# Turning the convolution's channels later: nine groups of transposes moved to the attention steps with few keys

## The reference, cut to what matters

```python
def conv_branch(u_ext, w, b, ln_g, ln_b):
    y = lax.conv_general_dilated(u_ext, w[:, None, :], ...) + b
    mu = jnp.mean(yf, axis=-1, keepdims=True)
    var = jnp.mean(jnp.square(yf - mu), axis=-1, keepdims=True)
    yn = (yf - mu) * lax.rsqrt(var + LN_EPS) * ln_g + ln_b
    return jax.nn.silu(yn)

mix = jnp.concatenate([conv_y * jax.nn.silu(gc), attn_o * jax.nn.silu(ga)], axis=-1)
out = x + mix @ w_out
```

## Time and profile before

| | |
|---|---|
| median of 3 runs | 1781.35 us |
| the profiled execution | 1779.65 us, its span 1778.0 us |
| PE busy | 1519.6 us, 85% of the span |
| DVE busy | 1042.7 us, 59% |
| ACT busy | 722.2 us, 41% |
| POOL busy | 487.1 us, 27% |
| mean granted clock of TensorE | 0.936 of full speed |
| third stage | about 957 to 1551 us of the span |

### The profile page before, as it was taken

The page is one execution under the profiler, slowest core; times in us unless marked ns, Lnnn a source line. Parts: engine busy times, 40 slices in busy tenths (PEclk is TensorE's granted clock), DMA queues, the critical chain, the costliest instruction groups (busy, mean ns, idle before and its releaser), DMA issues. The chain is left out here.

```text
span 1778.0 us, 28489 instructions
## 1 busy us (share of the span) xinstructions
PE 1519.6 (85%) x10637; PEld 1298.0 (73%) x10637; DVE 1042.7 (59%) x2135; ACT 722.2 (41%) x1302; POOL 487.1 (27%) x334
## 2 busy tenths in 40 slices
PE   5888999928979789999279999999999987549998
PEld 5786999927978669999257777776766765438886
DVE  2434999838988879898514444445544555343432
ACT  4445322224222252222124555556565654445431
POOL 2120333601434703355231011011223233141321
PEclk9999999969999899999668999999999998869999
DMA  7722442140346501232363034311121122294542
GB/s 241 223 74 48 101 120 74 47 86 30 90 136 224 162 1 49 68 103 68 113 179 85 21 90 109 70 40 33 44 67 42 53 67 66 75 228 143 167 149 98
DMA packets 183119, 172.72 MB, mean 97 GB/s; under 512 B 58974, under 2 KB 155366, under 8 KB 182462
## 3 DMA queue, kind: packets, MB, share of 16 engines
q1 hardware_dynamic: 180286, 165.14, 32.9%
q10 hardware_dynamic: 1672, 3.67, 1.3%
q0 software_dynamic: 1024, 2.10, 0.4%
HBM read 109.35 MB, written 58.19 MB: 94 GB/s over the span
## 5 line engine op out<-in xcount | busy, mean ns | idle before, releaser
L762 PE MATMUL psum<-xh,wh 128*128 128x384 f32 (+1 forms) x1040 | 343.1, 330 | 17.5 <-DMA xl<-d_xl 14.7
L762 PE MATMUL psum<-xh,wl 128*128 128x384 f32 (+1 forms) x1040 | 340.4, 327 | 0.0
L762 PE MATMUL psum<-xl,wh 128*128 128x384 f32 (+1 forms) x1040 | 340.3, 327 | 0.0
L1352 ACT ACTIVATE pts<-psT 128x512 f32<-128x512 f32 (+1 forms) x302 | 167.0, 572 | 264.7 <-PE psT L1653 242.6
L1532 DVE CUSTOM_DVE_ANT_0 L<-psU,mask 128x512 f32<-128x512 f32 (+3 forms) x260 | 143.5, 593 | 118.8 <-PE psU L1647 116.8
L762 PEld LDWEIGHTS psum<-xh,wh 128*128 128x128 f32 x1040 | 196.6, 189 | 19.8 <-issue 17.2
L1669 PE MATMUL psO<-pts,vs 128*64 128x128 f32 x2176 | 181.4, 288 | 26.9 <-ACT pts L1352 26.8
L762 PEld LDWEIGHTS psum<-xl,wh 128*128 128x128 f32 x1040 | 196.7, 189 | 0.0
L762 PEld LDWEIGHTS psum<-xh,wl 128*128 128x128 f32 x1040 | 196.5, 189 | 0.0
L893 DVE TENSOR_SCALAR_CACHE_REDUCE hit<-scores,T 128x1792 bf16<-128x1792 f32 (+8 forms) x120 | 184.6, 1539 | 11.7 <-issue 0.9
L1653 PE MATMUL psT<-cst,L 128*128 128x128 f32 x1105 | 171.3, 284 | 13.3 <-ACT L L1380 12.1
(11 more groups left out here) (268 smaller groups left out, 2624.9 us busy)
## 6 DMA issues: line engine op xcount, KB each, us to landing
wst<-in_w_in SPq DMA_DIRECT2D x28, 512.0 KB
wst<-in_w_in SPq DMA_DIRECT2D x32, 256.0 KB
qt<-d_q SPq DMA_DIRECT2D x16, 512.0 KB, 4.0
xst<-in_x_prompt SPq DMA_DIRECT2D x15, 512.0 KB, 3.8
xr<-in_x_prompt SPq DMA_DIRECT2D x15, 512.0 KB, 4.7
out_y_prompt<-fin SPq DMA_DIRECT2D x15, 512.0 KB, 2.9
gate<-d_ga SPq DMA_DIRECT2D x17, 256.0 KB, 4.3
d_mix<-mix SPq DMA_DIRECT2D x17, 256.0 KB, 2.2
```

Source lines behind the costliest of these rows:

```text
L762: last = nc.tensor.matmul(u[:, 0:k * P], a[:, w % 2, cc, :], x[:, s0:s0 + k, cc, :], start=(cc == 0 and e == 0), stop=(cc == KC - 1 and e ...
L1352: A.activation(out, src, ACT.Copy).then_inc(act_pt, 1)
```

## The change

The turns get a table of their own. `NORM_STEP` keeps the old steps (23, 27, ... 55) and drives `normalise` on DVE; `TURN_STEP` becomes 45, 47, ... 61 and drives everything that has to do with the turn: PE's matmuls, ACT's copies, the order of the jobs on the two banks of `psT`, and the place of SP's writes to `d_y`. Groups 0 to 8 are so turned at steps 45 to 61 in place of 23 to 55. Number and shape of all instructions stay.

```diff
 SQ_STEP = [s + 3 for s in SUM_STEP]
-TURN_STEP = [s + 5 for s in SUM_STEP]
+NORM_STEP = [s + 5 for s in SUM_STEP]
+
+TURN_STEP = [45 + 2 * k for k in range(len(NORM))]
+assert all(a >= b for a, b in zip(TURN_STEP, NORM_STEP))
...
                 for k in range(len(NORM)):
-                    if TURN_STEP[k] == p:
+                    if NORM_STEP[k] == p:
                         normalise(k)
```

## The result

The changed kernel takes 1790.41 us (median of 6 runs, 1788.83 to 1793.68). The kernel before, run beside it, takes 1782.01 us (6 runs, 1777.43 to 1783.83). The ratio is 1.0053, with a 95% interval from 1.0039 to 1.0067. The forecast was 1788.5 us in a range from 1780 to 1796. The profiled execution after took 1788.83 us with a span of 1787.2 us; it stands against 1779.65 and 1778.0 before. The third stage alone grew by 9.0 us (its end went from 1551.2 to 1560.2 us of the span).

What follows compares the result with a forecast made beforehand. Third stage bound by PE up to step 38, then in turned steps by the SP, mask, POOL, DVE, ACT chain. Terms -7.4 - 1.2 + 3.9 + 2.35 + 1.8 + 5.4 + 2.9 = +7.8 us; forecast 1788.5 us, range 1780 to 1796.

Steps and rivals of the forecast that it cites:

- early steps 23 to 35: Steps 23, 27, 31, 35: without the turn, PE's next transposes come earlier; -7.4 us together, 1.75 of it at step 31.
- steps 39 and 43: Exponentials are nearly the bound there already, so removing the turns gives only 0.55 and 0.65; together -1.2 us.
- half clock at steps 40 and 44: PE now waits 1.4 and 2.9 us there, so half clock may slow its work; +1.3 us for both.
- step 48, queue: SP's write of tile 16 delays the finished tile's write and loads 4.6 us; less PE's relief, +3.9 us.
- step 52, queue: SP's writes of turned tiles delay the finished tile's write at step 50 by 3.9 us; less PE's relief, +2.35 us.
- half clock behind both waits: Half clock now falls on transposes and products of steps 48 and 52, no longer on turns; 1.3 us each.
- turn at 53: New turn takes 1.8 us, 2.8 at half clock, 0.3 covered at step 55; +1.8 us, between 1.3 and 2.8.
- turns at 57, 59, 61: PE goes round without slack, so a turn at the step's end is paid in full: 3 x 1.81 = +5.4 us.
- Rival 1: SP's writes of turned tiles do not hold up the loads that matter; 1777 to 1781 us, no change; chance 0.10.
- Rival 4: DVE's wait for the inverse deviation still holds the next logits; PE's 8.7 us only show elsewhere. Held true, in the sum.
- Rival 2: Turns at 53 to 61 lie in PE's waits and cost nothing, queue delay absorbed; -10.9, 1769 to 1771 us; chance 0.06.
- Rival 3: Filled late steps keep full clock and the new waits do not lose it; +2.4, 1782 to 1784 us; chance 0.14.

Runs made afterwards that it cites:

- experiment 2: Changed kernel with another turn table: only group 5 moves, from step 43 to 45, the others turned as in the kernel before; 1786.89 us, ratio 1.0036.
- experiment 3: Changed kernel with another turn table: groups 0 to 5 turned as before, groups 6 to 8 at 57, 59, 61; 1789.19 us, ratio 1.0057.
- experiment 4: Kernel before, with POOL's inverse deviation put ahead of the mask and bias of the same step; 1762.58 us, ratio 0.9911.
- experiment 7: Changed kernel with POOL's inverse deviation ahead of its mask and SP's writes of turned tiles behind the loads; 1763.77 us, ratio 0.9911.
- experiment 1: Changed kernel with SP's writes of turned tiles behind the finished tile's write and the loads; 1778.76 us, ratio 0.9997.
- experiment 9: Changed kernel with the turn's first tile ahead of the step's last products at steps 47, 51, 55, 57, 59, 61; 1784.12 us, ratio 1.0023.

## Why the prediction was right, point by point

| step of the prediction | forecast | measured |
|---|---|---|
| early steps 23 to 35 | -7.4 | -8.5 |
| steps 39 and 43 | -1.2 | -0.4 and +0.25 |
| half clock at steps 40 and 44 | +1.3 of +2.9 | 0 and +0.35 |
| step 48, queue | +3.9 | +4.45 |
| step 52, queue | +2.35 | +3.1 |
| half clock behind both waits | +2.6 of +2.9 | +2.1 and +1.6 |
| turn at 53 | +1.8 | +0.3 |
| turns at 57, 59, 61 | +5.4 | +1.8, +1.8, +3.4 |
| end of the stage | -1 of +2.9 | -0.9 |
| sum | +7.8 | +9.0 |

(The measured column adds up with -0.3 more between steps 54 and 57.)

The mechanism is right and the sum is near, but in part by luck: some 4 us of misses upwards stand against 3 downwards. Two of the downward ones are chance of the execution before, which had stretches at half clock in steps 31 and 53. Experiments 2 and 3 have the same order of work up to step 42, and there step 31 takes 9.39 and 9.40 us where the trace before has 10.41; experiment 2 has the same order of work in step 53, and it takes 3.25 us where the trace before has 4.76:

```profile
1351.33:1360.72 9.39, 9.08 (x80) 7.07 (x80) 3.99 (x16) 6.11 (x11) 1.90 (x1) 1.00 0.03 9
...
1518.37:1521.62 3.25, 2.72 (x25) 2.27 (x26) 1.58 (x6) 2.13 (x7) 1.33 (x3) 1.00 0.21 77
```

(Experiment 3 has the slow stretch of step 53 too, experiment 4 has not.) So about 2.5 us of the downward misses belong to the execution before. Of the upward ones, 1.6 us are the half clock of step 61, which experiment 7 does not have. By groups of steps, the prediction gave -8, +6 and +7 for steps 23 to 44, 45 to 52 and 53 to 64; measured are -8.3, +11.3 and +6.1. The +6 left out the half clock that the sum has.

- **Early steps.** Right in kind. One is larger than forecast: step 31 gave 2.65 us in place of 1.75. Before, a stretch at half clock lies in that step, and it is not there after; by experiments 2 and 3 that is not the change's doing. Window of before (after, 1341 to 1344 has 1.00):

```profile
1344.00:1347.00 3.00, 3.00 (x18) 2.44 (x17) 2.90 (x11) 1.19 (x2) 0.00 (x0) 0.50 0.00 0
```

  Step 43 went the other way: its 0.65 us did not come. SP issued the load of the queries for tile 4 in 1.64 us in place of 0.43, so the loads behind it left later, DVE waited 8.29 us in place of 7.46, and the exponentials that the transposes of step 44 stand behind ended 8.1 us earlier than before, where all ahead of them had come 8.9 us earlier. Lines of before, then of after:

```profile
1428.25 0.43 SPq L1208 DMA_DIRECT2D qt<-d_q  x1
...
1440.90 1.23 DVE L1426 TENSOR_TENSOR yc<-yc,rs 128x1024 f32<-128x1024 f32 x1 [7.46 <-POOL rs L1332]
```

```profile
1419.32 1.64 SPq L1211 DMA_DIRECT2D qt<-d_q  x1
...
1432.80 1.23 DVE L1429 TENSOR_TENSOR yc<-yc,rs 128x1024 f32<-128x1024 f32 x1 [8.29 <-POOL rs L1335]
```

  Why that issue was long is open; experiments 1 and 9 have it too (1.70 and 1.32 us). PE's wait of 2.49 us in that step was followed by half clock (granted 0.50 from 1436 to 1438), which cost 0.35 us in step 44.

- **SP's order.** Forecast delays of the write: 4.6 and 3.9 us; measured 4.5 and 4.0. The delay passed down the chain in full, and 0.5 us more each time: `yc` moved by 5.0 and 4.5 us against the finished tile. (The prediction's own parts for the first delay, 2.03, 0.5 and 0.45 us behind 1457.28, add up to 4.4, not to 4.6.) SP's issues are longer than before (0.51 us for the write, against 0.33 in the earlier trace rows, and 0.68 for the mask, against 0.51 in the trace before). That addition is the part of the term that the prediction did not have. It goes with a write to `d_y` issued right ahead. In the late steps of the kernel before, the changed kernel and experiments 1, 2, 3 and 9, the finished tile's write took 0.50 to 0.56 us wherever SP came to it straight from a write to `d_y`, and 0.32 or 0.33 everywhere else. PE's relief was near the forecast: 0.6 for 0.7, and 1.4 for 1.55. DVE's idle time was to be about 12 us each time and was 10.66 and 11.32. Experiment 1 settles it: it took out the order and nothing else, and the whole 9.4 us (0.53% of 1782) were gone, the +7.6 of the two steps with half clock behind the first of them. In experiment 2 a single turn brought 5.5 us by this way.
- **A page's view of it.** The Trainium skill, "DMA: Bandwidth & Descriptors", Anatomy of one DMA — SWDGE (gpsimd) path, says that a DMA engine waits for no semaphore: the issuing sequencer does, before it dispatches. The section is on DMAs that GpSimd issues; the trace agrees for those of SP: `d_mix` goes 0.05 us behind the end of `d_y`, although the tile was finished 4.5 us before.
- **Rival 1 (delay absorbed)** fell with the same rows. **Rival 4 (renamed wait)** holds: 8.7 us became 10.8.
- **Late turns.** Steps 57 and 59 are right to 0.02 us. Step 61 costs 3.38 because the turn ran at half clock; I had priced it at full clock. Step 53 cost 0.3 in place of 1.8, by luck: before, that step was at half clock (granted 0.65), after it had the turn and full clock (1.00). Against the 3.25 us of experiment 2 the turn costs its 1.8. Windows from the transposes of step 53 to those of 54, before and after:

```profile
1506.30:1511.06 4.76, 4.23 (x25) 3.57 (x26) 1.83 (x8) 2.23 (x7) 2.83 (x3) 0.65 0.42 127
```

```profile
1509.25:1514.29 5.04, 4.51 (x41) 4.07 (x42) 1.58 (x6) 3.18 (x9) 3.10 (x3) 1.00 0.00 0
```

- **Rival 2 (the late steps have room)** fell in time, but its weak point was named rightly: the 0.75 us lie at another place in the step. Experiment 9 moved half of the work to that place, and 2.0 us of its cost went.
- **The clock.** The term's size was near, its parts less so. The stretches behind the two long waits were priced at 2.6 us together and cost 2.1 and 1.6; those at steps 40 and 44 were priced at 1.3 and cost 0.35; step 61 was priced at full clock. **Rival 3 (the clock comes back)** fell for the steps with waits, where the transposes took 1.94 us; the mean clock of the two profiled executions, 0.936 before and 0.933 after, shows no gain either. The Trainium skill, "TensorE: Matmul & The Clock Gate", What's actually happening, says that activity releases the throttle; by that I had priced a gain if work goes into idle steps. The traces do not bear that out. At steps 47 and 51 of the changed kernel the turns fill 2 us ahead of waits of up to 9, and the transposes behind them still run at half clock. Step 61 ran at full clock in experiment 9, with PE's wait filled, and in experiment 7, with it open. The page calls the ramp less than 1% of a typical kernel span. Here half clock decided up to 2 us in a step, several times, and that is much in a change worth 0.5% in all.

What stays open: why SP's issues take longer behind a write to `d_y`, and how the half-clock stretches would fall in another execution, since each profile is one execution. Steps 31, 53 and 61 show that they can fall otherwise for the same work.

## What to carry to other kernels

When an instruction is moved on one engine, follow its output to the queue that ships it, and ask what stands behind that entry: here three writes put ahead of the loads of two tiles gave back the whole gain of the early steps. A wait with a name is not yet a cost. The turns that waited 8.7 us for DVE sat in idle time and ran at half clock in place of what came behind them, while the real wait was the order of two pieces of work on POOL, worth 16 us (ratio 0.9911) and found by following the releasers back. And if work must go into late, short steps, put it into the gap (between the transposes and the products that wait for their copy), not beside it: 2.0 us of 5.4 here.

## What the runs showed of the hardware that I had not expected

Half clock moves with the work. Behind PE's waits of 5.27 and 6.01 us the first work, a turn, ran at it (3.78 us for 2.05, both times), and so did the transposes behind 7.62 and 8.97 us (1.97 and 1.94 us for 1.03). Behind waits of 3.07 and 3.41 us the logits still took their 0.47 us, and the transposes behind a second, shorter wait ran at half clock (1.94 and 1.97 us, and about 2 us over the step). Removing a piece of work behind such a wait so gives back less than its duration: at step 48 of experiment 3 nothing, once step 49 had started. Not every such stretch has a long wait ahead: at step 46 of the changed kernel the transposes took 1.93 us behind the turn of tile 16, and behind the same turn in experiment 1 they took 1.06. Step 61 with a whole turn behind its products had a granted clock of 0.67 in the changed kernel (5.22 us) and 1.00 in experiment 7 (3.63 us). What decides between the two is not shown by these runs. So a comparison of two single profiles of this kernel can have 1 to 1.6 us in a step that no edit made.
